# Reordered products in four places of a two-block transformer kernel: attention heads, pooling start, gate and up products, routing

## The reference, cut to what matters

```python
for l in range(2):
    if l == 0: x = x + pool_mixer(rms_norm(x, ..), ..)     # trailing-window means, per-group linear
    else:                                                  # latent attention, 8 heads
        s = (q_nope @ k_nope.T + q_rope @ k_rope.T) * ATTN_SCALE   # 128 + 64 columns
        p = softmax(where(mask, s, -inf)); x = x + concat(p @ v) @ wo
    x = x + hier_moe(rms_norm(x, ..), ..)                  # 4 groups x 8 experts, top 2 of a group
x = rms_norm(x, final_norm)
for l in range(2):                                         # 2 x (FFN, mixer, FFN)
    x = x + 0.5 * rmsnorm(swiglu(rmsnorm(x)))              # silu(h @ w_gate) * (h @ w_up) @ w_out, width 2816
    x = x + rmsnorm(mixer(rmsnorm(x)))                     # differential attention + mLSTM
    x = x + 0.5 * rmsnorm(swiglu(rmsnorm(x)))
```

## Time and profile before

| | |
|---|---|
| median of three runs | 2056.9 us (2054.51 to 2061.02) |
| the profiled execution | 2053.74 us |
| span of its instructions | 2051.9 us |
| TensorE busy | 1942.2 us, 95% |
| VectorE busy | 878.8 us, 43% |
| ScalarE busy | 671.5 us, 33% |
| HBM read | 594.78 MB, 290 GB/s over the span |
| mean granted TensorE clock | 0.989 of full |

### The profile page before, as it was taken

One profiled execution on the slowest core, in us unless ns is written; L12 is line 12 of the kernel. 1 busy time (PEld: TensorE's weight loads), 2 busy tenths in 40 slices (PEclk: granted clock), 3 DMA queues, 4 the chain that ended last, 5 costly groups with the idle time before them and its releaser, 6 DMA issues. The chain is left out here.

```text
span 2051.9 us, 36391 instructions
## 1 busy us (share of the span) xinstructions
PE 1942.2 (95%) x16088; PEld 1382.5 (67%) x16088; DVE 878.8 (43%) x1395; ACT 671.5 (33%) x1138; POOL 60.5 (3%) x97
## 2 busy tenths in 40 slices
PE   7999989988999999999989999999999999999998
PEld 5644444445875444444458888878888888887887
DVE  4111111104651111111156656875655665786663
ACT  2000000004440000000054546674545554675552
POOL 0000000000000000000020000010000000011000
PEclk8999999999999999999999999999999999999999
DMA  9999999998769999999976545336555655425551
GB/s 411 385 428 429 430 428 429 430 427 365 267 246 424 429 429 430 429 429 428 429 288 217 189 171 186 127 125 220 186 183 191 210 187 185 164 96 187 187 192 68
DMA packets 56767, 598.33 MB, mean 292 GB/s; under 512 B 6291, under 2 KB 6803, under 8 KB 9747
## 3 DMA queue, kind: packets, MB, share of 16 engines
q1 hardware_dynamic: 55444, 592.44, 71.8%
q10 hardware_dynamic: 1152, 3.41, 0.5%
HBM read 594.78 MB, written 1.05 MB: 290 GB/s over the span
## 5 line engine op out<-in xcount | busy, mean ns | idle before, releaser
L1979 DVE TENSOR_TENSOR SPLIT<-RING,SPLIT 128x2048 fp32r<-128x2048 f32 (+2 forms) x178 | 398.8, 2255 | 141.2 <-ACT SPLIT L1457 140.9
L1126 PE MATMUL PS<-HTB,SPLIT 128*128 128x512 f32 x1152 | 406.3, 398 | 0.0
L759 PE MATMUL PS<-RING,WK 128*32 128x512 f32 x816 | 362.8, 598 | 35.7 <-DVE WK L2248 26.9
L1457 ACT ACTIVATE SPLIT<-RING 128x2048 fp32r<-128x2048 f32 (+2 forms) x178 | 332.6, 1888 | 46.0 <-DMA RING<-in_units 46.0
L1127 PE MATMUL PS<-HTB,SPLIT 128*128 128x256 f32 x1152 | 322.5, 280 | 0.0
L759 PEld LDWEIGHTS PS<-RING,WK 128*32 128x32 f32 x816 | 86.0, 110 | 275.1 <-issue 235.1
L1126 PEld LDWEIGHTS PS<-HTB,SPLIT 128*128 128x128 f32 x1152 | 216.4, 188 | 52.6
L1605 ACT ACTIVATE WK<-PS 128x128 f32<-128x128 f32 x64 | 17.7, 277 | 678.5 <-PE PS L725 678.5
L1127 PEld LDWEIGHTS PS<-HTB,SPLIT 128*128 128x128 f32 x1152 | 217.3, 189 | 0.2
L725 PE MATMUL PS<-RING,WK 128*32 128x128 f32 x5696 | 187.2, 277 | 5.5 <-issue 4.2
L725 PEld LDWEIGHTS PS<-RING,WK 128*32 128x32 f32 x5696 | 162.8, 110 | 29.1 <-issue 25.0
(11 more groups left out here) (341 smaller groups left out, 2339.6 us busy)
## 6 DMA issues: line engine op xcount, KB each, us to landing
RING<-in_units SPq DMA_DIRECT2D x171, 1024.0 KB, 4.8
RING<-in_w_down SPq DMA_DIRECT2D x53, 2048.0 KB, 31.9
RING<-in_w_gate SPq DMA_DIRECT2D x45, 2048.0 KB, 29.5
RING<-in_w_up SPq DMA_DIRECT2D x44, 2048.0 KB, 32.4
WK<-in_w_up SPq DMA_DIRECT2D x17, 2048.0 KB, 33.5
WK<-in_w_gate SPq DMA_DIRECT2D x16, 2048.0 KB, 31.8
WK<-in_w_down SPq DMA_DIRECT2D x6, 2048.0 KB, 35.2
SEAT<-in_w_up SPq DMA_DIRECT2D x3, 2048.0 KB, 26.7
```

The lines of the kernel that those rows point to most:

```text
L759: t = pe.matmul(PS[32 * i:32 * i + 32, 4 + h, :], mo.HE[:, pb, 32 * f:32 * f + 32], v[:, c, 512 * h:512 * h + 512], start=f == 0, stop=f == 3)
L1126: pe.matmul(out.rearrange("p (z b n) -> p z b n", z=2, b=2), wh, HTB[:, :, :, c, :], start=start, stop=False)
L1457: ac.activation(unit_part(u, 0), loaded(u), ACT.Copy).then_inc(s_hi, 1)
L1979: dv.tensor_tensor(unit_part(u, 1), loaded(u), unit_part(u, 0).bitcast(F32), ALU.subtract).then_inc(s_lo, 1)
```

## The change

Five edits, in which nothing of what is computed changes.

1. Attention. The rope part of the keys, `KR` (64 rows, held twice, in partitions 0 to 63 and 64 to 127), becomes `KZ`, two copies of 128 rows: one for the even heads with zeros below, one for the odd heads with zeros above. The rope product now contracts 128 rows, with the queries of a pair of heads. GpSimd clears `KZ` in a memset; VectorE writes the halves in two adds instead of one. Scores are made three heads ahead of values. VectorE takes a head's low part (`values`) before the division of a later one (`weigh`). Of the splits of units 11, 12 and 13, which were two behind head 3 and one behind head 5, one comes behind head 3, one behind head 5 and one behind the last head of the loop, on ScalarE and VectorE.
2. Pooling. ScalarE issues the two row transfers as its first instructions, instead of SyncE as its fifth and sixth. The row of ones is made by a GpSimd memset in SM and not read from the transferred constants, for which TensorE then waits later. VectorE adds block 0 of the pooled result when its last product is done (`s_po` at 7), not that of both blocks (8).
3. Gate and up. `wide` makes the eight 512-column products, then waits for `s_lo`, then makes the eight 256-column products. At the start of a unit the wait is for `s_hi`.
4. Routing of moe1. `keep_warm(pe, 0, 8)` instead of 4.
5. Waits on `s_mh` are renumbered for the added memsets.

```diff
@@ -350,7 +350,7 @@
         ml.QR = al(1024).rearrange("p (h n) -> p h n", h=4)
-        ml.KR = al(256)
+        ml.KZ = al(512).rearrange("p (z n) -> p z n", z=2)
         ml.PT = al(768).rearrange("p (k n) -> p k n", k=2)
@@ -400,6 +400,8 @@
+        ONE = SM[0:1, 384:512]
+
         def gate_weights(l, z):
@@ -479,10 +481,6 @@
             sp.dma_start(CS[:, 0:NCST0], W["cst"][:, 0:NCST0]).then_inc(s_cs, 16)
-
-            a, b = ROWS["pool_b"][0], ROWS["r0"][0]
-            sp.dma_start(HT[0:1, :, :].rearrange("p c n -> p (c n)"), W["rows"][0:1, a:a + 2048]).then_inc(s_first, 16)
-            sp.dma_start(RB[0:1, 2, 0:80], W["rows"][0:1, b:b + 80]).then_inc(s_first, 16)
             for k, stage in enumerate(STAGES):
@@ -534,8 +532,9 @@
                 po.tensor_tensor(out, out, MH[:, 0:out.shape[1]], ALU.pow).then_inc(done, 1)
+            po.memset(ONE, 1.0).then_inc(s_mh, 1)
             po.memset(MH[:, :], -0.5).then_inc(s_mh, 1)
-            po.wait_ge(s_mh, 1)
+            po.wait_ge(s_mh, 2)
@@ -554,6 +553,7 @@
                 if stage == "mla":
+                    po.memset(ml.KZ, 0.0).then_inc(s_mh, 1)
                     for z, size in ((0, 256), (2, 384)):
@@ -623,11 +623,13 @@
+            pe.wait_ge(s_mh, 1)
             pe.wait_ge(s_first, 32)
...
             for k in range(4):
-                pe.matmul(PS[:, 4 + k, :], cs("ones")[0:1, :], rows[:, 512 * k:512 * k + 512], start=True, stop=True)
-            pe.matmul(PS[:, 3, 0:80], cs("ones")[0:1, :], RB[0:1, 2, 0:80], start=True, stop=True).then_inc(s_pg, 1)
+                pe.matmul(PS[:, 4 + k, :], ONE, rows[:, 512 * k:512 * k + 512], start=True, stop=True)
+            pe.matmul(PS[:, 3, 0:80], ONE, RB[0:1, 2, 0:80], start=True, stop=True).then_inc(s_pg, 1)
+            pe.wait_ge(s_cs, 16)
             pe.wait_ge(s_xsa, 2)
@@ -676,7 +678,7 @@
-                keep_warm(pe, 0, 4)
+                keep_warm(pe, 0, 8)
@@ -996,7 +998,7 @@
             def scores(h):
-                bk, pr, dp = h % 2, h // 2, 64 * (h % 2)
+                bk, pr = h % 2, h // 2
                 pe.wait_ge(s_lata, 11 + h // 2)
@@ -1010,7 +1012,7 @@
                     pe.matmul(o, ml.QN[:, h, i * 128:i * 128 + 128], ml.KN[:, h, 0:m], start=True, stop=False)
-                    pe.matmul(o, ml.QR[dp:dp + 64, pr, i * 128:i * 128 + 128], ml.KR[dp:dp + 64, 0:m], start=False,
+                    pe.matmul(o, ml.QR[:, pr, i * 128:i * 128 + 128], ml.KZ[:, h % 2, 0:m], start=False,
                               stop=True).then_inc(s_sc, 1)
@@ -1059,12 +1061,13 @@
             rotate(3)
+            scores(2)
             for h in range(8):
...
                     break
-                if h < 6:
-                    scores(h + 2)
+                if h < 5:
+                    scores(h + 3)
                 values(h)
@@ -1120,11 +1123,14 @@
-        def wide(pe, out, weights, c, start, stop):
-
-            wh, wl = weights
-            pe.matmul(out.rearrange("p (z b n) -> p z b n", z=2, b=2), wh, HTB[:, :, :, c, :], start=start, stop=False)
-            return pe.matmul(pair(out[:, 0:256]), wl, HTH[:, :, c, :], start=False, stop=stop)
+        def wide(pe, out, hi, lo, low):
+
+            for c in range(8):
+                pe.matmul(out.rearrange("p (z b n) -> p z b n", z=2, b=2), hi(c), HTB[:, :, :, c, :], start=c == 0, stop=False)
+            low()
+            for c in range(8):
+                t = pe.matmul(pair(out[:, 0:256]), lo(c), HTH[:, :, c, :], start=False, stop=c == 7)
+            return t
@@ -1142,9 +1148,9 @@
                     hi, lo = unit_pair(u)
-                    pe.wait_ge(s_lo, u + 1)
+                    pe.wait_ge(s_hi, u + 1)
                     for fq in range(2):
-                        f = 2 * fp + fq
+                        f, cols = 2 * fp + fq, slice(fq * 128, fq * 128 + 128)
                         if fp == 2 and fq:
@@ -1153,9 +1159,8 @@
                             pe.wait_ge(s_hfl, 20 * i + 2)
-                        for c in range(8):
-                            t = wide(pe, PS[:, ffn_bank(f, z), :],
-                                     (hi[:, c, fq * 128:fq * 128 + 128], lo[:, c, fq * 128:fq * 128 + 128]), c, c == 0, c == 7)
+                        t = wide(pe, PS[:, ffn_bank(f, z), :], lambda c: hi[:, c, cols], lambda c: lo[:, c, cols],
+                                 lambda: pe.wait_ge(s_lo, u + 1))
                         if fq:
@@ -1423,7 +1428,6 @@
         def tensor_program(pe):
-            pe.wait_ge(s_cs, 16)
             pe_pool(pe)
@@ -1441,6 +1445,9 @@
             junk = [None]
+            a, b = ROWS["pool_b"][0], ROWS["r0"][0]
+            ac.dma_start(HT[0:1, :, :].rearrange("p c n -> p (c n)"), W["rows"][0:1, a:a + 2048]).then_inc(s_first, 16)
+            ac.dma_start(RB[0:1, 2, 0:80], W["rows"][0:1, b:b + 80]).then_inc(s_first, 16)
@@ -1749,9 +1756,9 @@
                         hi(11)
+                    elif h == 5:
                         hi(12)
-                    elif h == 5:
-                        hi(13)
+                hi(13)
                 values(7)
@@ -2087,8 +2094,8 @@
                 dv.tensor_tensor(X[:, 1, :], X[:, 1, :], RB[:, 0, :], ALU.add).then_inc(own.up(), 1)
-                dv.wait_ge(s_po, 8)
-                for b in range(2):
+                for b in range(2):
+                    dv.wait_ge(s_po, 7 + b)
                     j = XS[:, b, :]
@@ -2354,11 +2361,13 @@
                 dv.wait_ge(s_lata, 1)
-                dv.tensor_tensor(ml.KR, ml.TQ[:, 0, :], cos, ALU.mult).then_inc(own.up(), 1)
                 dv.wait_ge(s_latp, 1)
+                dv.tensor_tensor(ml.TQ[:, 0, :], ml.TQ[:, 0, :], cos, ALU.mult).then_inc(own.up(), 1)
                 dv.tensor_tensor(ml.R2, PS[:, 5, 256:512], sin, ALU.mult).then_inc(own.up(), 1)
                 settle()
-                dv.tensor_tensor(ml.KR, ml.KR, ml.R2, ALU.add).then_inc(s_latv, 1)
+                dv.wait_ge(s_mh, 3)
+                dv.tensor_tensor(ml.KZ[0:64, 0, :], ml.TQ[0:64, 0, :], ml.R2[0:64, :], ALU.add).then_inc(own.up(), 1)
+                dv.tensor_tensor(ml.KZ[64:128, 1, :], ml.TQ[64:128, 0, :], ml.R2[64:128, :], ALU.add).then_inc(s_latv, 1)
                 for c in range(2):
@@ -2424,16 +2433,18 @@
                 weigh(1)
+                scores(2)
                 for h in range(7):
+                    if h < 5:
+                        scores(h + 3)
+                    values(h)
                     if h < 6:
-                        scores(h + 2)
                         weigh(h + 2)
-                    values(h)
                     if h == 3:
                         lo(11)
+                    elif h == 5:
                         lo(12)
-                    elif h == 5:
-                        lo(13)
+                lo(13)
                 values(7)
```

More of the change, by code:

```diff
@@ L1591, in moe @@
                 ac.activation(mo.EE, mo.DD, ACT.Exp).then_inc(s_ee, 1)
-                ac.wait_ge(s_mh, 1)
+                ac.wait_ge(s_mh, 2)
                 ac.activation(SM[0:1, 200 + l:201 + l], MH[0:1, 0:1], ACT.Silu)
@@ L1870, in sums @@
                                (s_nsq, 8 * l + 2 * h + b + 1))
-                ac.wait_ge(s_mh, 3)
+                ac.wait_ge(s_mh, 5)
                 for z in range(2):
```

## The result

Six runs of the kernel after gave 2041.46 to 2044.59 us, median 2042.42; six of the kernel before on the same chip 2051.36 to 2061.02, median 2055.63. The ratio is 0.9938, 95% interval 0.9922 to 0.9953: faster, by 13 us. A second group of runs on another chip has 2043.73 against 2055.21, ratio 0.9943 (0.993 to 0.9957). The forecast was 2043, range 2038 to 2050.

The account below looks back on a forecast made before the run. Transfers with holes were taken to bound moe0 and moe1, TensorE the second block. Pooling 3.8, attention 4.8 and gate and up 4.8 make 13.4 us less; from the median 2056.9 that is 2043.5, said as 2043, range 2038 to 2050.

Parts of the forecast that it names:

- Pooling, rows earlier: In pooling, ScalarE issuing the row transfers first starts TensorE's first product, and so the first mean, 2.9 us earlier.
- Pooling, block 0: In pooling, VectorE adds block 0 without waiting for block 1's last two products, so the chain comes 0.86 us earlier.
- the hole: Idle 4.2 us in the transfer stream between 40 and 60 us; pooling's gain of 3.8 us was to pass whole.
- Attention: 128-row rope products and scores three heads ahead gain about 4.8 us at the end of attention; bounds 1.5 and 6.5.
- Rival 2: In attention, heads gain only idle time, 1.5 us, as the 64 rows or the chain limit it; 2046.8 us, chance 0.14.
- The splits moved: In attention, splits of 2.3 us each on VectorE stay covered behind the output products, 5.4 us each.
- Gate and up: In the FFN stages, grouping products by length removes 0.0072 us per pair in three stages; term 4.8 us, range 0 to 7.5.
- rival 4: In gate and up, the wait between the runs bares a weight load of about 0.12 us per group; 2065.6 us, chance 0.04.
- my last paragraph: Signs in the changed profile: FFN distances of 0.227 and 0.119 us; 0.235 in the first run means the four-piece pattern costs.
- Rival 1: In the FFN stages, order is free and the term is 0; 8.6 us less in all, 2048.3 us, chance 0.16.
- Routing: At moe1's routing, four more products just fit TensorE's idle 1.73 us; 0 gained, at most 0.2 us lost.
- The sum: Whole kernel: 3.8 for pooling, 4.8 for attention and 4.8 for gate and up make 13.4 us less.

Follow-up runs that it names:

- u_pool: The kernel after with only the pooling edit undone; its time was 3.3 us above a repeat of the kernel after, 5.8 by the ratios.
- b_again: The kernel before, unchanged, run and profiled again; gate and up parts lasted 102.4, 102.5, 100.7 and 102.5 us, first scores came at 541.51 us.
- u_mla: The kernel after with 64-row rope products, scores two heads ahead and the old order and splits; median 2050.45 us, attention stage 52.49.
- rows64: The kernel after with only the rope product back at 64 rows; 5.0 us above a repeat of the kernel after, attention stage 51.88 us.
- two_ahead: The kernel after with scores two heads ahead and the old order and splits; 2.8 us above a repeat of the kernel after, attention stage 51.15.
- u_alt: The kernel after with only the gate and up edit undone, so 512- and 256-column products alternate again; 2047.39 us, second block 972.25.

## Why the prediction was right, point by point

**Pooling, rows earlier.** Mechanism right, the size 2.2 instead of 2.9 us: the rows took 3.66 us from their issue at 1.30, where I had 3.2 from 1.1. The last step, 7.44 us from the first product to the first mean, is the same to 0.01 us.

**Pooling, block 0.** 0.86 as said: 1.63 of idle time became 0.77, and 1.63 again in u_pool.

**That it passes through the hole.** Right up to its size. Two executions tested the hole beyond it: expert 0 began 5.7 (b_again) and 7.3 us (u_mla) earlier than in the profile before, and the first scores came 3.7 and 4.1 us earlier. That fits the 4.2 us of the earlier trace rows, at which the stream takes over: in both the transfers are busy all the time from 40 to 60 us (share 1.01). The other side of it the prediction didn't say: in an execution whose clock has filled the hole without the edit, as in b_again, the edit has nothing to gain.

**Attention.** Term 4.8, measured 5.8. The 0.68 us per head are 0.67, and the weight loads that no product covers are in the trace of rows64. The loop is 2.16 to 2.40 us and not 2.45: the low part and the next scores filled all of VectorE's wait for the exponentials. I took the idle time of TensorE, at most 2.6 us, and the row cost as terms that add. They do not; rows64 and two_ahead show two bounds at 3.08 and 3.24 us per head. The 3.39 from which the working started was the longest of three heads (3.25, 3.39, 3.25). Rival 2 would have had the chain take what TensorE saves, and that is what happens in two_ahead, without the new order. The splits moved cost nothing: they stand behind the quarters of the output product in the trace of after, as said.
The rule of the Trainium skill (TensorE: Matmul & The Clock Gate, table of "Why this matters for your kernels"), that a small contraction takes the time of a full one, doesn't describe this place: the scores took 1.98 and 1.31 us for the same columns. The 64-row product does take as long as the 128-row one beside it; what the rule leaves out is that both become slower.

**Gate and up.** The term that was mis-sized: 4.8 us forecast, 2.8 to 2.9 measured, inside its range of 0 to 7.5. Three stages went from 102.4 and 102.5 to 101.3 (3.5 us), the quick one from 100.7 to 101.3 (0.6 lost). "A change of length remains twice per group, 144 groups x 0.0072" was wrong: the excess of one group is 20 ns and not 7, spread over the five products behind the change, 144 x 0.020 = 2.9 us in all and not 1.0. The other part was a little too large as well: by start times a slow pair costs 353.3 ns and the two pure rates 346.7, so three stages could give 3 x 288 x 0.0067 = 5.8 us and not 6.2, and 5.8 - 2.9 is the 2.9 measured. The waits cost nothing that can be seen, and of rival 4 there is no trace: the step from the last 512-column product to the first 256-column one is 226.7 ns, the pure pace, in all 144 groups. The 512-column mean of 0.231 us in the first run is not the four-piece operand's cost, as my last paragraph would have had it for 0.235: the last three products of each run have the same pattern and take 226.7 ns.
Rival 1 falls: u_alt and after differ by nothing but the order and, with it, the places of the waits for `s_hi` and `s_lo`, and the second block takes 972.25 against 969.3 us.

**Routing.** No idle time is left, as said, and the products just fit (a quarter us spare). "The clock is up anyway, so 0 gained" was true of the profile before, but not of every execution: b_again took 2.8 us more there. What that is worth on the median isn't shown.

**The sum.** By the profiled pair, without moe1's 2.35: 2.8 (pooling, at the first scores) + 5.8 (attention) + 3.0 (second block) = 11.6 us, with routing in some executions 1.6 to 2.8 more, against 13.4 forecast and 12 to 13 measured by the two groups of runs. That 2043 was forecast and 2042.42 measured is in part luck: pooling was 1.0 and gate and up 1.9 too much, attention 1.0 too little, and the first group's 13.2 us is more than the stages account for.

## What to carry to other kernels

Where engines hand work to each other in a loop, find two lengths: the busiest engine's own work, and the chain of waits from engine to engine. If they are close, as 3.08 and 3.24 us here, an edit to either alone looks almost worthless (0.6 and 1.3 us of the stage) and only the pair shows the gain (5.8). When products of two lengths alternate, look at distances from start to start over a whole stage, not at one stage and not at durations: group as many of one length as the buffers allow, and price each change of length by a run of the group itself. Here the quick rhythm of the plain alternation (100.7 us a stage) beats both groupings (101.3 and 101.0); no run shows how to hold it in all four stages. A gain ahead of a stream of transfers is worth its size only up to the hole that the stream has there, which can be read off the busy share of the transfers before anything is tried, in more than one profile, since the clock fills the hole in some.

## What was not expected of the hardware

TensorE's alternation of 512 and 256 columns has two steady rhythms, 353.3 and 346.7 ns per pair, each held for some 260 pairs, and a small disturbance ahead, such as one more 128-column transpose, decides between them; it repeats from execution to execution (the same stage was quick in before, b_again and u_alt). Why there are two, and why a run of 512 columns behind one of 256 loses 27 ns over five products and gives back 8 at the next change, stays open.
